# Where three activation tiles start beside their weight tiles, in a two-block float32 kernel

## The chip, the core and the metric

The kernel runs on one core of a Trainium2 chip. The metric is the device time of one launch in microseconds; lower is better. The kernel before took 1932.09 us (median of 3 runs, 1929.77 to 1934.56).

## The reference

Two model blocks run one after the other over 256 tokens of width 1024, in float32. The first has a recurrent layer (a gated linear recurrence beside a state-space part), a gated feed-forward network, an attention layer with three dilated windows, and a second network. The second block has two layers; each multiplies its normed input by a 1024 x 12240 matrix, feeds three branches (latent attention, RWKV, gated linear attention) and merges them. What matters here is that nearly all weight is in plain products. The feed-forward network:

```python
def swiglu_layer(x, norm_g, w_gate_up, w_down):      # 1024 -> 2 x 2816 -> 1024
    h = rmsnorm(x, norm_g)
    g, u = jnp.split(h @ w_gate_up, 2, axis=-1)
    return x + (jax.nn.silu(g) * u) @ w_down
```

and the input of each layer of the second block:

```python
        h = _rms_norm(x, norm_pre[l]) * (1 + scale[:, None, :]) + shift[:, None, :]
        p = h @ w_in[l]
```

## The kernel before

Activations lie features first: a tile of 8 rows of 256 tokens (DK x T, 4 bytes each), so a product is out = weights^T x activations with a 128x128 weight tile held in TensorE (a weight load, PEld) and 256 token columns moving past it (a matmul). Most products are made in three passes of the faster fp32r type: weights and activations are each split into a rounded part ("high") and the rest ("low"), and high x high, high x low and low x high are added in one bank. Each pass loads its weight tile again. In a product "by token" (line 697) the roles are turned: the activations are the held tile and 256 weight columns move.

Weights stream through two layouts. In the layers a weight unit of 8 x 128 columns (UNIT, 4096 bytes a partition) lands in one of five raw buffers, ScalarE or VectorE rounds it into one of three high buffers (lines 722, 717), VectorE writes the low part over the raw one (line 733), and TensorE multiplies (`multiply_unit`, line 708; `first_units_by_pieces`, line 667, for the first two units of a stage). In the two networks (`ffn_pe`) bigger pieces go through two slots of high and low parts in the tile `parts`; the first half of a network (gate and up) multiplies the networks' input rows H_PARTS, the second half (down) the inner rows HIDDEN_PARTS, both by `three_passes` (lines 1486 to 1488) in hardware loops, with the first piece of the first half at line 1501.

Three places are set by constants in words of 4 bytes. X_SHIFT: the layer input HX (high and low) begins that many words after the start of a room behind the high buffers. H_SHIFT: H_PARTS begins that many words behind the weight slots in `parts`. HIDDEN_SHIFT: the same for HIDDEN_PARTS. All rooms, units and slots are multiples of 256 bytes long, so these constants are also the distance, modulo 256 bytes, between any row of the three tiles and any weight tile that it is multiplied with: 64, 64 and 192 bytes.

Used so: HX feeds every three-pass product of the recurrent layer's input and of both layers' inputs in the second block (by token at line 697 for one of them); H_PARTS feeds the networks' first halves and the attention layer's query, key and value products; HIDDEN_PARTS feeds the networks' second halves. By the code's units (24 matmuls to a unit of 8 tiles, 48 to a piece of a network's first half, 132 to a turn of its second half) these are 4968, 2688 and 1056 matmuls, 8712 together, of 10,536 in three passes. The other 1824 (outputs of the branches, expansions of the latent attention) have tiles at other distances, which the change leaves alone: among them the RWKV output (192 bytes), the recurrent layer's second output half (0 and 128) and the last output product of a layer (high part 64, low part 0).

Of the kernel before, what the change touches and what calls it, by code (L numbers as in the profile page):

```python
# [163 lines left out]
def program(nc, A, out, stop=None):  # L164
    with ExitStack() as ctx:
# [16 lines left out]
        KD_ = FFN // P  # L182
        UNIT, RAWS, HIGHS = DK * P, 5, 3
        LINE = 128
        X_SHIFT, H_SHIFT, HIDDEN_SHIFT = (16, 16), (16, 16), (48, 48)
        WHOLE = 2 * KD_ * COLS + 2 * 2 * T + LINE
        SPLIT_AT, SPLIT = COMMON + WHOLE, 2 * 2 * DK * COLS + 2 * DK * T + 2 * KD_ * T + 2 * LINE
        psum = [ctx.enter_context(nc.psum_tensor(f"bank{i}", [P, 512], F32))[:, :] for i in range(8)]
# [3712 lines left out]
```

How the kernel before makes its waits and increments, by code:

```python
        def load_first_up(l):  # L560
            sp.wait_ge(unit_used.sem, last_split[l] + 1)
            for s in range(2):
                for to, frm in ffn_up[l].loads(s, WHOLE_UP[s]):
                    sp.dma_start(to, frm).then_inc(landed[s].sem, 16)
# [1 line left out]
        def load_up(l):  # L567
            job, turns = ffn_up[l], turns_before[l]
            with sp.Fori(1, UPS) as j:
                for s in range(2):
                    sp.wait_ge(lo_ready[s].sem, j + turns)
                    for to, frm in job.loads(j * 2 + s, WHOLE_UP[s]):
                        sp.dma_start(to, frm).then_inc(landed[s].sem, 16)
# [1 line left out]
        def load_down(l):  # L575
            job, turns = ffn_down[l], turns_before[l]
            for q in range(2):
                sp.wait_ge(lo_ready[q].sem, turns + UPS)
                for to, frm in job.loads(q, WHOLE_DOWN[q]):
                    sp.dma_start(to, frm).then_inc(landed[q].sem, 16)
            with sp.Fori(1, DK // 2) as j:
                for q in range(2):
                    sp.wait_ge(lo_ready[1].sem, j * 2 + (turns + UPS + q - 1))
                    for to, frm in job.loads(j * 2 + q, WHOLE_DOWN[q]):
                        sp.dma_start(to, frm).then_inc(landed[q].sem, 16)
# [46 lines left out]
        def load_units(job):  # L632
# [1 line left out]
                u = job.first + i  # L634
                if u >= RAWS:
                    sp.wait_ge(unit_used.sem, u - RAWS + 1)
                for to, frm in job.loads(i, UNIT_RAW[u % RAWS].rearrange("p (k c) -> p k c", k=job.kt)):
```

## Time and profile before

| | |
|---|---|
| median of 3 runs | 1932.09 us |
| profiled execution, its own time | 1930.44 us |
| its span (first to last instruction) | 1927.4 us |
| outside the span | 3.0 us |
| TensorE busy with matmuls | 1849.3 us, 96% |
| VectorE busy | 1339.1 us, 69% |
| ScalarE busy | 814.6 us, 42% |
| mean granted TensorE clock | 0.991 of full |

A matmul's own duration (about 280 ns) is longer than the distance from one to the next (under 120 ns), since they are pipelined. What a product costs is therefore read from how many matmuls start in a stretch: in a window of L microseconds without a stall that is wholly covered, the count holds also those that began up to 0.28 us before it, so the distance is (L + 0.28) / count.

### The profile page before, as it was taken

The numbers are of one execution on the slowest core, as the hardware profiler recorded it, in microseconds if no ns is written. First come the engines' busy times: TensorE is split into PE (matmuls) and PEld (weight loads), VectorE is DVE, ScalarE is ACT, GpSimd is POOL, SyncE is SP. The second block draws the span as 40 slices with busy tenths as digits, with TensorE's granted clock in tenths as the row PEclk, the third lists the DMA queues.
The fourth block names the chain that finished last, engine by engine and source line by source line (L and its number), as shares of the span: only waits on it lengthen the run. The fifth ranks groups of instructions, "written<-read, shape, count | busy, mean of one in ns | idle before, by whom it ended". The sixth has DMA issues, their size and how long they took to land.

```text
span 1927.4 us, 42678 instructions
## 1 busy us (share of the span) xinstructions
PE 1849.3 (96%) x18447; PEld 1728.3 (90%) x18447; DVE 1339.1 (69%) x1723; ACT 814.6 (42%) x1219; POOL 88.3 (5%) x131
## 2 busy tenths in 40 slices
PE   8999999999899999999998999998999999999999
PEld 7987999998689999998987799897998997889988
DVE  8897688757748876764786469666774696459755
ACT  5573534435634342223755234254213664235154
POOL 2000000000400000002000000000002000000000
PEclk9999999999999999999999999999999999999999
DMA  8555477974337795663550145554563651135644
GB/s 224 144 144 152 129 264 257 271 201 137 105 99 250 264 267 136 164 174 94 163 153 15 47 119 165 145 146 128 145 185 88 163 154 47 28 105 160 172 118 134
DMA packets 473228, 291.94 MB, mean 151 GB/s; under 512 B 26775, under 2 KB 467580, under 8 KB 472872
## 3 DMA queue, kind: packets, MB, share of 16 engines
q1 hardware_dynamic: 466720, 262.13, 48.5%
q0 software_dynamic: 5312, 25.32, 3.5%
q10 hardware_dynamic: 1032, 2.11, 0.5%
q8 instruction: 126, 2.06, 0.5%
q14 instruction: 38, 0.31, 0.1%
HBM read 287.95 MB, written 1.05 MB: 150 GB/s over the span
## 4 chain that ended last, share of the span: by engine, by line
PE 79%; DVE 14%; ACT 4%; issue 2%; DMA 1%; ACTq 0%; POOL 0%; DVEq 0%
PE bank L708 37%; PE bank L1486 6%; PE bank L1488 6%; PE bank L1487 6%; DVE rounded L733 4%; PE bank L667 3%; PE bank L949 3%; PE bank L697 2%; ACT rounded L722 1%; PE bank L1692 1%; PE bank L1679 1%; PE bank L1116 1%; DVE rounded L717 1%; PE bank L790 1%; PE bank L941 1%
## 5 line engine op out<-in xcount | busy, mean ns | idle before, releaser
L708 PE MATMUL bank<-rounded 128*128 128x256 f32 x5928 | 719.1, 281 | 10.2 <-DVE rounded L733 7.9
L708 PEld LDWEIGHTS bank<-rounded 128*128 128x128 f32 x5928 | 700.8, 187 | 25.2 <-DVE rounded L733 12.3
L733 DVE TENSOR_TENSOR rounded<-arena,rounded 128x1024 fp32r<-128x1024 f32 (+1 forms) x307 | 370.6, 1215 | 102.5 <-ACT rounded L722 94.6
L1486 PE MATMUL bank<-parts 128*128 128x256 f32 x1024 | 287.2, 280 | 1.0 <-DVE parts L2323 0.9
L1488 PE MATMUL bank<-parts 128*128 128x256 f32 x1024 | 285.9, 279 | 0.0
L1487 PE MATMUL bank<-parts 128*128 128x256 f32 x1024 | 285.6, 279 | 0.0
L722 ACT ACTIVATE rounded<-arena 128x1024 fp32r<-128x1024 f32 x192 | 201.5, 1057 | 170.2 <-PE bank L708 103.5
L1486 PEld LDWEIGHTS bank<-parts 128*128 128x128 f32 x1024 | 192.8, 188 | 2.2 <-issue 1.2
L1488 PEld LDWEIGHTS bank<-parts 128*128 128x128 f32 x1024 | 192.3, 188 | 0.0
L1487 PEld LDWEIGHTS bank<-parts 128*128 128x128 f32 x1024 | 192.1, 188 | 0.1
L773 ACT ACTIVATE arena<-bank 128x512 f32<-128x512 f32 x90 | 53.2, 596 | 241.6 <-PE bank L708 227.7
L2395 ACT ACTIVATE parts<-whole 128x2048 fp32r<-128x2048 f32 x44 | 84.3, 1918 | 126.9 <-PE bank L1488 109.4
L717 DVE CAST rounded<-arena 128x1024 fp32r<-128x1024 f32 (+1 forms) x115 | 78.2, 680 | 69.2 <-PE bank L708 43.0
L2315 DVE TENSOR_TENSOR parts<-whole,parts 128x2048 fp32r<-128x2048 f32 x44 | 100.7, 2292 | 16.8 <-ACT parts L2395 16.1
L708 PE MATMUL bank<-arena 128*128 128x256 f32 x416 | 91.1, 379 | 0.0
L949 PE MATMUL bank<-common,arena 128*128 128x128 f32 x519 | 78.1, 285 | 13.3 <-DMA common<-in_const 7.1
L708 PEld LDWEIGHTS bank<-arena 128*128 128x128 f32 x416 | 78.9, 190 | 11.5 <-issue 1.0
L708 PE MATMUL bank<-common,arena 128*128 128x256 f32 x384 | 87.8, 383 | 0.0
L708 PEld LDWEIGHTS bank<-common,arena 128*128 128x128 f32 x384 | 71.2, 189 | 10.9 <-issue 0.3
L949 PEld LDWEIGHTS bank<-common,arena 128*128 128x128 f32 x519 | 58.6, 145 | 23.0 <-DMA common<-in_const 7.1
L2323 DVE TENSOR_TENSOR parts<-whole,parts 128x1408 fp32r<-128x1408 f32 x32 | 52.0, 1625 | 38.9 <-ACT parts L2427 38.8
L2427 ACT ACTIVATE parts<-whole 128x1408 fp32r<-128x1408 f32 x32 | 44.1, 1380 | 65.9 <-PE bank L1488 54.5
(407 smaller groups left out, 2405.8 us busy)
## 6 DMA issues: line engine op xcount, KB each, us to landing
arena<-in_w_in SPq DMA_DIRECT2D x190, 512.0 KB, 3.8
whole<-in_ffn_w_gate_up SPq DMA_DIRECT2D x44, 1024.0 KB, 5.2
arena<-in_ada_w POOLq DMA_DIRECT2D x32, 768.0 KB, 6.4
whole<-in_ffn_w_down SPq DMA_DIRECT2D x16, 1408.0 KB, 7.2
arena<-in_rec_w_in SPq DMA_DIRECT2D x36, 512.0 KB, 3.8
arena<-in_att_w_qkv SPq DMA_DIRECT2D x24, 512.0 KB, 3.8
arena<-in_rec_w_out SPq DMA_DIRECT2D x16, 512.0 KB, 3.7
arena<-in_mla_w_o SPq DMA_DIRECT2D x16, 512.0 KB, 3.7
```

The source lines that it names most:

```text
L667: last = pe.matmul(psum[s][:, i * T:i * T + T], w[a][:, kk, :], job.rhs[b][:, kk, :], start=(i, kk, a, b) == (0, 0, 0, 0), stop=kk == job. ...
L708: last = pe.matmul(psum[s][0:c, m % 2 * T:m % 2 * T + T], w[a][:, k, cols], x[b][:, k, :], start=(k, a, b) == (0, 0, 0), stop=k == job.kt ...
L717: write(high_view(job_of[u], u), raw_view(job_of[u], u, UNIT_RAW)).then_inc(done.sem, 1)
L722: high_parts(act, lambda to, frm: act.activation(to, frm, ACT.Copy), high_by_act[0].pop(0), unit_high_s)
L733: dve.tensor_tensor(raw_view(job_of[u], u, UNIT_LOW), raw, high_view(job_of[u], u).bitcast(F32), ALU.subtract)\
L773: return lambda i, bank, done, rounds: act.activation(two(dst, i, lo), bank, func).then_inc(done, 1)
L949: last = pe.transpose(bank[:, n * P:n * P + P], x, ident)
L1486: pe.matmul(bank, w_hi, x_hi, start=start and k == 0, stop=False)
L1487: pe.matmul(bank, w_hi, x_lo, start=False, stop=False)
L1488: last = pe.matmul(bank, w_lo, x_hi, start=False, stop=stop and k == n - 1)
L2315: dve.tensor_tensor(UP_W[s][1], WHOLE_UP[s], UP_W[s][0].bitcast(F32), ALU.subtract)\
L2395: act.activation(UP_W[s][0], WHOLE_UP[s], ACT.Copy)\
```

## The change

Three constants change. X_SHIFT goes from 16 to 12 words (64 to 48 bytes), H_SHIFT from 16 to 4 (64 to 16 bytes), HIDDEN_SHIFT from 48 to 52 (192 to 208 bytes), each for the high and the low part alike. Every instruction, its size and its place in each engine's order stay; only the start addresses of HX, H_PARTS and HIDDEN_PARTS change, for those who write them (ScalarE and VectorE) and for TensorE, which reads them. All starts stay multiples of 16 bytes; they are no longer multiples of 64.

```diff
--- before.py
+++ after.py
@@ -182,7 +182,7 @@
         KD_ = FFN // P
         UNIT, RAWS, HIGHS = DK * P, 5, 3
         LINE = 128
-        X_SHIFT, H_SHIFT, HIDDEN_SHIFT = (16, 16), (16, 16), (48, 48)
+        X_SHIFT, H_SHIFT, HIDDEN_SHIFT = (12, 12), (4, 4), (52, 52)
         WHOLE = 2 * KD_ * COLS + 2 * 2 * T + LINE
         SPLIT_AT, SPLIT = COMMON + WHOLE, 2 * 2 * DK * COLS + 2 * DK * T + 2 * KD_ * T + 2 * LINE
         psum = [ctx.enter_context(nc.psum_tensor(f"bank{i}", [P, 512], F32))[:, :] for i in range(8)]
```

## Rows read from the trace of the kernel before

**Rows 1.** The page: span, engines, TensorE's granted clock by slice.

```profile
span 1927.4 us, 42678 instructions
...
PE 1849.3 (96%) x18447; PEld 1728.3 (90%) x18447; DVE 1339.1 (69%) x1723; ACT 814.6 (42%) x1219; POOL 88.3 (5%) x131
...
PEclk9999999999999999999999999999999999999999
```

**Rows 2.** The page's chain that ended last: shares by line.

```profile
PE bank L708 37%; PE bank L1486 6%; PE bank L1488 6%; PE bank L1487 6%; DVE rounded L733 4%; PE bank L667 3%; PE bank L949 3%; PE bank L697 2%; ACT rounded L722 1%; PE bank L1692 1%; PE bank L1679 1%; PE bank L1116 1%; DVE rounded L717 1%; PE bank L790 1%; PE bank L941 1%
```

**Rows 3.** Groups by line and shape, TensorE (count; busy, mean ns; idle before).

```profile
L708 PE MATMUL bank<-rounded 128*128 128x256 f32 x5856 | 710.8, 281 | 10.2 <-DVE rounded L733 7.9 <-ACT arena L773 1.6 <-ACT common L3280 0.6
L1486 PE MATMUL bank<-parts 128*128 128x256 f32 x1024 | 287.2, 280 | 1.0 <-DVE parts L2323 0.9
L708 PE MATMUL bank<-arena 128*128 128x256 f32 x416 | 91.1, 379 | 0.0
```

**Rows 4.** Windows without a stall, TensorE: stretch, length, busy (count), clock, DMA.

```profile
core 0: us, PE busy (x), PEclk, DMA share, GB/s
233.00:333.00 100.00, 100.00 (x852) 1.00 0.74 252
353.00:368.00 15.00, 15.00 (x134) 1.00 1.05 312
675.50:684.50 9.00, 9.00 (x82) 1.00 1.01 270
693.00:743.00 50.00, 50.00 (x427) 1.00 0.98 277
789.50:801.00 11.50, 11.50 (x104) 1.00 0.51 141
1381.00:1398.00 17.00, 17.00 (x147) 1.00 0.64 168
1173.00:1181.00 8.00, 8.00 (x73) 1.00 0.66 193
195.50:206.00 10.50, 10.50 (x91) 1.00 0.66 189
1315.00:1328.00 13.00, 13.00 (x111) 1.00 0.79 220
```

**Rows 5.** Timeline, one network's first half, then second half, TensorE.

```profile
239.84 0.28 PE L1488 MATMUL bank<-parts 128*128 128x256 f32 x1
239.95 0.28 PE L1486 MATMUL bank<-parts 128*128 128x256 f32 x1
...
359.96 0.28 PE L1487 MATMUL bank<-parts 128*128 128x256 f32 x1
360.07 0.28 PE L1488 MATMUL bank<-parts 128*128 128x256 f32 x1
```

**Rows 6.** Windows over three of eight quick stretches of moved products, TensorE.

```profile
137.40:142.60 5.20, 5.20 (x49) 1.00 0.53 158
352.40:399.60 47.20, 47.20 (x413) 1.00 1.03 302
...
1795.40:1817.00 21.60, 21.60 (x193) 1.00 0.70 187
```

**Rows 7.** Windows over three networks' halves: length, then PE PEld DVE ACT POOL, clock, DMA.

```profile
220.50:346.20 125.70, 125.61 (x1062) 125.27 (x1060) 96.00 (x86) 49.23 (x39) 5.28 (x10) 1.00 0.70 235
346.20:407.80 61.60, 61.24 (x528) 60.68 (x529) 43.91 (x40) 28.36 (x28) 7.02 (x8) 1.00 0.93 271
...
685.80:748.80 63.00, 62.44 (x530) 62.27 (x530) 43.15 (x36) 23.56 (x19) 2.11 (x4) 1.00 0.86 243
```

**Rows 8.** Waits of TensorE: total us, times, longest.

```profile
PE bank L708 <- DVE rounded L733: 9.0, 13, 1.4
```

**Rows 9.** Timeline, two full-precision stages with other row positions, TensorE.

```profile
151.78 1.46 PE L708 MATMUL bank<-arena 128*128 128x256 f32 x6
...
997.76 2.11 PE L708 MATMUL bank<-common,arena 128*128 128x256 f32 x9
```

## Prediction

> **What bounds the kernel now.** I read the page first. TensorE is busy for 96% of the 1927.4 us span, and its granted clock is the full level, 2.4 GHz, in all 40 slices [rows 1]. In the chain that ended last, line 708 holds 37% of the span and the three passes of the networks 6% each [rows 2]. So the end is set by how fast one three-pass matmul follows the other, and by little else: the largest wait of TensorE behind the product stream, that for VectorE's low parts, is 9.0 us in 13 waits [rows 8]. Two of the groups show the size of the stream: 5856 matmuls at line 708 take 710.8 us, 121.4 ns each with all their small stops, and each of the three passes of the networks has 1024 [rows 3].
>
> The change moves no instruction. It can act only through the distance between matmuls, so the reader has to look at that distance by stage. From the windows (length plus 0.28 us, over the count) it comes out in two levels [rows 4]:
>
> - first network's first half (64 bytes): 100.28 / 852 = 117.7 ns
> - the same network's second half (192 bytes): 15.28 / 134 = 114.0
> - end of the second network's first half (64): 9.28 / 82 = 113.2
> - second network's second half (192): 50.28 / 427 = 117.8
> - two stages on HX (64): 11.78 / 104 = 113.3 and 17.28 / 147 = 117.6
> - RWKV output, not moved (192): 8.28 / 73 = 113.4
> - recurrent output (128 and 0): 10.78 / 91 = 118.5
> - a layer's last product (high 64, low 0): 13.28 / 111 = 119.6
>
> The timeline shows the same at single matmuls: starts at 239.84 and 239.95 in the one, and at 359.96 and 360.07 in the other, where over a longer run the first goes at about 118 and the second at about 113 [rows 5].
>
> Two things follow. One distance knows two steady levels, 113.3 (quick) and 117.8 (slow): the same code at the same addresses ran its second half quick in the first network and slow in the second. So something other than the address picks the level, and it holds until the stream is interrupted. But the address has a part in it. Where 0 or 128 is mixed in, I find neither level but 118.5 and 119.6, and by length the quick level is far more common at 192 than at 64. Eight quick stretches of the moved products hold 1,271 matmuls, from the one at 137.4 to the one at 1795.4; the longest, 413 matmuls in 47.2 us with its small stops, is a second half at 192 [rows 6].
>
> **The change part by part.** Removed and added instructions: none. Written tiles: ScalarE and VectorE write HX, H_PARTS and HIDDEN_PARTS as often and as long as before; I cost their new starts at nothing, since VectorE is busy for only 96.0 of the 125.7 us of a network's first half [rows 7], and if it did get slower there it has 30 us of room. Moved reads: 4968 matmuls on HX, 2688 on H_PARTS, 1056 on HIDDEN_PARTS, 8712 in all. About 1,271 of them are quick and 7,441 slow.
>
> *Does a start off a multiple of 64 bytes cost by itself?* The full-precision stages answer for starts inside the granule. At 152 us the tokens' rows start at 48 past a multiple of 64 (by the layout), and six records take 1.46 us; the last has its own 379 ns at the end [rows 3], so (1.46 - 0.38) / 5 = 216 ns. At 998 us the rows start 12 past one, and nine take 2.11 us: (2.11 - 0.38) / 8 = 216 ns [rows 9]. That stream needs its rows at half the rate, so it bounds the cost only for a slow reader: from below 0, from above unknown. I take 0 and keep in the range one quarter of the step between the levels, 1.1 ns x 8712 = 10 us.
>
> *Which level do the moved streams take?* No row shows 48, 16 or 208. The nearest rows are 64, 192 and 0. They bound one matmul from both sides. Below: the quick level everywhere, 7,441 x (117.8 - 113.3 = 4.5 ns) = 33 us gained. Above: the price of 0. In the last product one matmul in three has 0, so it costs (119.6 - 117.7) x 3 = 5.7 ns. Weighed by nearness to 0, that is 1.4 ns for HX (48 lies three quarters of the way to 64), 4.3 for H_PARTS (16), 1.4 for HIDDEN_PARTS (208): 4968 x 1.4 + 2688 x 4.3 + 1056 x 1.4 = 7.0 + 11.6 + 1.5 = 20 us, and the quick matmuls of today would be lost too, 1,271 x 4.5 = 5.7 us: 26 us lost.
>
> Between these ends I choose the side of the quick level. All distances met so far are multiples of 64 bytes, and at those the stream sits on the edge between two levels: the same addresses give both. Which of two steady patterns comes out is then a matter of how the weight reads and the token reads fall between each other in time; a distance inside the granule shifts one against the other by a part of a step, and a tie that the grid of 64 leaves open need not be open there. I take two thirds of the moved matmuls as quick: 5,808 - 1,271 = 4,537 more, x 4.5 = 20 us. This is a choice, not a reading.
>
> *What is given back.* A quicker TensorE meets its suppliers earlier. The two second halves price it: the one that was mostly quick (413 x 4.5 = 1.9 us to gain) took 61.6 us, the slow one 63.0 [rows 7], so 1.4 of 1.9 us was kept, three quarters. The rest is late weights: DMA was busy 0.93 of that window. Of 20 us I keep 15. From the profiled execution's own 1930.4 us (1.7 below the median) that gives 1915 us.
>
> The page "SBUF — State Buffer" of the Trainium skill says in "Who interferes with whom" that TensorE has two independent read ports, one for the moving operand and one for the weight load, and waits on nobody. By it the distance could not matter and the sum would be 0. The rows at mixed 0 and 128 stand against it, the two levels at one address stand beside it unexplained.
>
> **The rivals.** *Nothing happens* (1931): the level is picked by the moment of the last interruption alone, and the address is only along for the ride. For it: quick and slow at the same 64 and at the same 192. Against it: the second halves and the branch outputs at 192 are quick so much more often. Each interruption draws anew, so the sum would wander by a few us: 1925 to 1937. It is also what the page's rule would give.
>
> *The tiles come too close to their weights* (slower, 1946). One mechanism: the nearer to a distance of 0, the more often the token read meets the weight read in the same place, as in the last product. It bites at H_PARTS first, at 16 bytes, which is all of the networks' first halves. Its full price is the 26 us above; since the recurrent output, with 0 in a third of its matmuls too, shows 118.5 and not 119.6 (0.8 x 3 = 2.4 ns in place of 5.7, under half), I take three fifths, 16 us. It decides from the point where a matmul at 16 bytes costs over 1 ns. For it: both stages with 0 are above both levels. Against it: only about a third of the sum is from distances that were seen, and 48 and 208 are still nearer to the old places.
>
> *Everything gets quick* (1905): 33 us, three quarters kept, 25 us. I count it to my forecast's case, at its edge.
>
> *A third level below 113.3* (about 1865): 256 columns at 2.4 GHz are 106.7 ns, so up to 7,441 x 11 + 1,271 x 6.6 = 90 us, three quarters kept. For it only that 113.3 is itself not the floor; no row of this type shows less.
>
> **How the numbers follow.** Quick for a good part of the moved matmuls: 0.44 (1905 to 1924). A third level: 0.05. Nothing: 0.23. Too close: 0.28. What a measurement of this kernel can tell from no change is about 0.3%, 6 us. Faster: 0.42 of the first case, 0.05, and 0.03 of wandering, 0.50; same: 0.02 + 0.18 + 0.02 = 0.22; slower: 0.02 + 0.26 = 0.28. The range leaves out the third level, the upper end of the full price at 0, and takes in the rest: 1897 to 1948. The likeliest case's own range is 1905 to 1924.
>
> **What would show it.** Right: windows in the networks' first halves (both slow now for nearly their whole 125 us) with counts near 883 in 100 us in place of 852, their length near 121 us, and HX stages at 113.3; waits for VectorE's low parts a little above 9 us. Wrong in the choice: counts of 852 again, or new distances of 118.5 and more, most of all in the first halves at 16 bytes. Wrong in the give-back: quick windows everywhere, but the halves no shorter. If HX, H_PARTS and HIDDEN_PARTS answer differently, the three distances have to be told apart, and my one share for all of them was wrong. VectorE's and ScalarE's mean durations should not move at all.

## The result, and the profile after

The changed kernel is slower: 1936.57 us (median of 11 runs, 1932.37 to 1941.55) against 1929.89 for the kernel before in its 11 runs; ratio 1.0031, 95% interval 1.0021 to 1.0042. The forecast was 1915, in a range of 1897 to 1948. Four executions in the groups below, two of them of the kernel before, took 2650 to 6351 us and are left out of every ratio.

Page of the changed kernel: span, busy times of the engines, chain that ended last by line.

```profile
span 1934.8 us, 42678 instructions
...
PE 1858.8 (96%) x18447; PEld 1739.4 (90%) x18447; DVE 1339.2 (69%) x1723; ACT 815.1 (42%) x1219; POOL 88.3 (5%) x131
...
PE bank L708 39%; PE bank L1486 6%; PE bank L1488 6%; PE bank L1487 6%; DVE rounded L733 3%; PE bank L949 3%; PE bank L667 3%; PE bank L697 2%; PE bank L1692 1%; PE bank L1679 1%; PE bank L1116 1%; ACT rounded L722 1%; DVE rounded L717 1%; PE bank L1660 1%; PE bank L941 1%
```

Against [rows 1] TensorE is busy for 9.5 us more and idle for 76.0 us in place of 78.1; 9.5 - 2.1 = 7.4 us, which is the whole growth of the span. VectorE, ScalarE and GpSimd are busy as before to within 0.5 us. In the chain line 708 grows from 37% to 39% [rows 2].

Groups by line and shape, and the wait that [rows 8] shows, after:

```profile
L708 PE MATMUL bank<-rounded 128*128 128x256 f32 x5856 | 716.3, 283 | 9.3 <-DVE rounded L733 7.2 <-ACT arena L773 1.6 <-ACT common L3280 0.6
L1486 PE MATMUL bank<-parts 128*128 128x256 f32 x1024 | 288.4, 282 | 1.1 <-DVE parts L2323 1.1
L708 PE MATMUL bank<-arena 128*128 128x256 f32 x416 | 91.1, 379 | 0.0
```

```profile
PE bank L708 <- DVE rounded L733: 7.9, 11, 1.4
```

The same 5856 matmuls take 5.5 us more than in [rows 3], the full-precision ones exactly as long as before, and the wait for VectorE's low parts is shorter, 7.9 us in place of 9.0, as it would be if TensorE comes later and finds its suppliers in time more often.

Windows without a stall after, TensorE: stretch, length, busy (count), clock, DMA share, GB/s.

```profile
229.00:265.00 36.00, 36.00 (x311) 1.00 0.65 216
270.00:330.00 60.00, 60.00 (x508) 1.00 0.73 250
356.00:378.00 22.00, 22.00 (x187) 1.00 0.96 287
423.00:435.00 12.00, 12.00 (x108) 1.00 0.62 182
570.00:670.00 100.00, 100.00 (x845) 1.00 0.70 241
693.00:749.00 56.00, 56.00 (x472) 1.00 0.91 257
793.00:811.00 18.00, 18.00 (x154) 1.00 0.57 157
```

With the formula of [rows 4] the first network's first half (H_PARTS at 16 bytes) runs at 116.7 ns, then at 118.7; the second network's at 118.7 (845 matmuls in 100 us, where the kernel before had 852 and the forecast wanted 883); the second halves (208 bytes) at 119.1 and 119.2; attention's first product on H_PARTS (16) at 113.7; a stage on HX (48) at 118.7, which is 118.35 by its starts. The granted clock is 1.00 in all of them, 2.4 GHz. So these are new levels, not a new mix of the two old ones.

**The granted clock.** It is not at the full level throughout. The page's digits hide it, but the trace of the kernel before has six short stretches, 34 us together, at 0.50 (1.2 GHz), in which three-pass matmuls start 213 ns apart. One of them begins at 756.5 us, after TensorE had run 48 matmuls of one column each (line 1551, from 752.3 us on), and covers a layer's first products; below it an equal length at 1.00:

```profile
756.60:763.30 6.70, 6.70 (x32) 0.50 0.06 20
1380.00:1386.70 6.70, 6.70 (x60) 1.00 0.44 108
```

The profiled execution of the changed kernel has 34 us of this too, so the busy times above compare fairly. Over all executions the mean clock is 0.9903 for the changed kernel and 0.9917 for the 29 of the kernel before that ran beside the first experiments. Within the groups an execution with 0.001 less of clock takes about 0.9 us more, so some 1 us of the 7 may be the clock's; this is an estimate from these numbers. Why the clock fell a little more often is not shown.

The networks' halves after: length, then PE PEld DVE ACT POOL, clock, DMA.

```profile
220.90:346.90 126.00, 126.00 (x1062) 125.65 (x1061) 96.08 (x85) 49.19 (x38) 5.28 (x10) 1.00 0.71 235
346.90:411.10 64.20, 63.67 (x533) 63.29 (x532) 44.05 (x40) 28.45 (x28) 7.01 (x8) 1.00 0.89 259
687.40:751.30 63.90, 63.37 (x532) 63.20 (x531) 43.15 (x36) 23.60 (x19) 2.11 (x4) 1.00 0.84 238
```

By the first and last start the two second halves take 63.8 and 63.6 us; before, 61.5 and 62.9 [rows 7]. The new distance explains it: 528 x 119.17 ns = 62.9 us, and the rest is small stops.

**Where the time went, by tile.** One matmul more or less in a window of 18 us is 0.8 ns, which is too coarse. For the tables I took from the trace's records every three-pass matmul whose next three follow without a pause, and averaged the distance of their starts; the stretches at 1.2 GHz are left out. "Quick" is the share within 1.7 ns of 113.3.

| stream | matmuls | before: distance, ns, quick | after | sum |
|---|---|---|---|---|
| HX | 4584 | 64: 117.28, .11 | 48: 118.26, .01 | +4.5 us |
| HX by token (roles turned) | 384 | 192: 115.08, .61 | 208: 118.05, 0 | +1.1 |
| H_PARTS, networks | 2112 | 64: 117.58, .04 | 16: 118.33, 0 | +1.6 |
| H_PARTS, attention | 384 | 64: 117.78, 0 | 16: 115.86, .46 | -0.7 |
| H_PARTS, attention by token | 192 | 192: 114.75, .68 | 240: 118.34, 0 | +0.7 |
| HIDDEN_PARTS | 1056 | 192: 115.92, .42 | 208: 119.15, 0 | +3.4 |

Together +10.6 us of stream, of which the span shows 7.4. The streams that were not moved agree: 117.56 and 117.78 at 64, 116.01 and 116.16 at 192. A single short stream wanders more, though: the RWKV output, at 192 in every kernel that leaves the weight units in place, has quick shares from .18 to .98 (before .49, after .35). In the product by token the weight columns move and the activations are held, so the distance has the other sign; the prediction counted these 576 matmuls with the rest and did not say so. The 4584 on HX also hold 72 with weight tiles of only 16 columns, whose distances run through the multiples of 64.

### The profile page after: what moved, and what is told of

It is laid out like the page before. It is cut to its first block, busy times and chain, and to the rows that moved or that the text cites. A ratio compares the mean times of both kernels' runs of the same rounds, so it can differ in the third digit from the quotient of the medians.

```text
span 1934.8 us, 42678 instructions
## 1 busy us (share of the span) xinstructions
PE 1858.8 (96%) x18447; PEld 1739.4 (90%) x18447; DVE 1339.2 (69%) x1723; ACT 815.1 (42%) x1219; POOL 88.3 (5%) x131
## 4 chain that ended last, share of the span: by engine, by line
PE 80%; DVE 12%; ACT 3%; issue 2%; DMA 1%; ACTq 0%; POOL 0%; DVEq 0%
PE bank L708 39%; PE bank L1486 6%; PE bank L1488 6%; PE bank L1487 6%; DVE rounded L733 3%; PE bank L949 3%; PE bank L667 3%; PE bank L697 2%; PE bank L1692 1%; PE bank L1679 1%; PE bank L1116 1%; ACT rounded L722 1%; DVE rounded L717 1%; PE bank L1660 1%; PE bank L941 1%
## 5 line engine op out<-in xcount | busy, mean ns | idle before, releaser
L717 DVE CAST rounded<-arena 128x1024 fp32r<-128x1024 f32 (+1 forms) x115 | 78.1, 679 | 73.1 <-PE bank L708 43.6
```

The costliest lines, as they stand in the source:

```text
L717: write(high_view(job_of[u], u), raw_view(job_of[u], u, UNIT_RAW)).then_inc(done.sem, 1)
```

## The experiments

All of them move tiles and no instruction. Where there is an interval, the kernel before ran beside it in the same rounds.

### One tile at a time

```diff
-        X_SHIFT, H_SHIFT, HIDDEN_SHIFT = (16, 16), (16, 16), (48, 48)
+        X_SHIFT, H_SHIFT, HIDDEN_SHIFT = (12, 12), (16, 16), (48, 48)   # only HX, 48 bytes
+        X_SHIFT, H_SHIFT, HIDDEN_SHIFT = (16, 16), (4, 4), (48, 48)     # only H_PARTS, 16
+        X_SHIFT, H_SHIFT, HIDDEN_SHIFT = (16, 16), (16, 16), (52, 52)   # only HIDDEN_PARTS, 208
```

> Only the layer input HX moves (64 to 48 bytes); H_PARTS stays at 64, HIDDEN_PARTS at 192. Theory A (each stream's level is set by its own distance): every stall-free window on HX shows 118.3 ns between matmuls in place of 117.8 or 113.3, all else as before; 4968 x 0.55 ns = 2.7 us, and about 700 quick matmuls lost x 5 ns = 3 us: 5 to 6 us slower, ratio about 1.003, nearly all of the change. Rival (the levels are redrawn by chance at each stall, the distance only rides along): HX windows show 113.3 or 117.8 again in other places, and the ratio lies within 1.001 of 1.

> Only the networks' input H_PARTS moves (64 to 16 bytes). Theory A: in the networks' first halves neither 117.8 nor 113.3 shows, but the new levels of 16 bytes, 116.7 and 118.7; per network half (1056 matmuls) between -1.2 and +0.9 us. Since 118.7 holds for longer, in all -1 to +2 us, ratio 1.000 to 1.001. It is also the part whose runs spread most (116.7 against 118.7 over 2016 matmuls is 4 us). Rival (chance alone): 117.8 as before over nearly all of both first halves, ratio 1.000.

> Only the inner rows HIDDEN_PARTS move (192 to 208 bytes). Theory A: both second halves run at about 119 ns and never at 113.3; against before 1056 x 1.3 ns = 1.4 us and 413 quick matmuls more x 4.4 ns, three quarters of it kept: together 2 to 3 us slower, ratio 1.0013. Rival (chance alone): one second half or both show 113.3 stretches again, ratio within 1.001 of 1.

| moved alone | median, us | before, us | ratio, 95% interval |
|---|---|---|---|
| HX to 48 | 1934.42 | 1929.29 | 1.0025 [1.0016, 1.0034] |
| H_PARTS to 16 | 1929.58 | 1929.29 | 0.9999 [0.9988, 1.0010] |
| HIDDEN_PARTS to 208 | 1932.18 | 1929.29 | 1.0018 [1.0008, 1.0028] |

The parts' sum is 1.0042, the whole 1.0031, within each other's intervals. HX has 118.26 ns again, with no quick stretch, as theory A has it. H_PARTS, the tile nearest to its weights, costs nothing here. Its windows say why; networks with H_PARTS alone at 16:

```profile
229.00:265.00 36.00, 36.00 (x311) 1.00 0.67 222
268.00:323.00 55.00, 55.00 (x460) 1.00 0.74 250
326.00:345.00 19.00, 19.00 (x170) 1.00 0.88 271
568.00:604.00 36.00, 36.00 (x311) 1.00 0.65 219
630.00:672.00 42.00, 42.00 (x362) 1.00 0.75 255
```

116.7, 120.2, 113.4, 116.7 and 116.8 ns: at 16 bytes the same loop knows four levels (118.7 is the fourth, after), changes between them where the stream is interrupted, and here they average 117.45, about as 64 bytes did (117.58). The expectation had left out 113.3 and 120.0, and in the trace of the change, where 118.7 held for longer, the same distance had 118.33. With HIDDEN_PARTS alone at 208, the second halves:

```profile
356.00:371.00 15.00, 15.00 (x128) 1.00 1.02 302
695.00:749.00 54.00, 54.00 (x465) 1.00 0.93 261
```

119.4 and 116.7 ns: two levels again, neither of them 113.3; the expectation had about 119 for both.

### All three at 192

```diff
+        X_SHIFT, H_SHIFT, HIDDEN_SHIFT = (48, 48), (48, 48), (48, 48)
```

> HX, H_PARTS and HIDDEN_PARTS all stand at 192 bytes, a multiple of 64 (so HX and H_PARTS move from 64). Theory A (distance 192 reaches the quick level more readily than 64): more than half of the moved matmuls at 113.3, that is some 3500 more x 4.4 ns, three quarters kept: 10 to 13 us faster, ratio 0.994. Rival (level redrawn by chance at stalls, the same for 64 and 192): about one in seven quick as before, ratio within 1.001 of 1.

1921.98 us, ratio 0.9959 [0.9943, 0.9976]: faster than both kernels, though by 7 us and not by the 10 to 13 expected. Its page and four windows (first network's first half, second network's, its second half, a stage on HX):

```profile
span 1918.9 us, 42678 instructions
...
PE 1835.6 (96%) x18447; PEld 1714.3 (89%) x18447; DVE 1338.1 (70%) x1723; ACT 815.0 (42%) x1219; POOL 88.3 (5%) x131
```

```profile
229.00:345.00 116.00, 116.00 (x987) 1.00 0.73 244
632.00:682.00 50.00, 50.00 (x444) 1.00 0.81 267
690.00:745.00 55.00, 55.00 (x469) 1.00 0.92 258
765.00:783.00 18.00, 18.00 (x161) 1.00 0.77 181
```

117.8, 113.2, 117.9 and 113.5 ns: only the two old levels, but mixed otherwise. HX has 114.84 ns with .66 quick (64 gave .11), the networks' first halves 116.68 with .25. TensorE's busy time falls by 13.7 us and the span by 8.5, 62%; some 1.5 us of either is the clock, which is at 1.2 GHz for 31 us here and for 34 before (an estimate from the two distances, 213 and 118 ns). Its wait for the low parts is longer:

```profile
PE bank L708 <- DVE rounded L733: 11.2, 19, 1.5
```

### Distance or start?

The change moves two things at once: the distance and the place of the rows in the granule of 64 bytes. Two kernels keep one of them. All unit buffers of the layers start 48 bytes past a multiple of 64 and HX 64 bytes behind them (first), or the unit buffers start at 16 and HX at 48 bytes behind, so that its rows are on a multiple of 64 (second).

```diff
+        OFF = [0]
...
-            place[0] += (COMMON - place[0]) % 16
+            place[0] += (COMMON + OFF[0] - place[0]) % 16
...
+        OFF[0] = 12        # second: 4, and X_SHIFT = (12, 12)
```

> The weight units of the layers start 48 bytes past a multiple of 64, and HX with them (112 bytes past), so their distance stays 64 as before while the rows of HX start off a multiple of 64, as after the change. H_PARTS in its own products with `parts` and HIDDEN_PARTS are untouched. Theory A (the distance between row and weight tile decides): windows on HX show 117.8 or 113.3 ns as before. Rival (a row that starts off a multiple of 64 bytes is read more slowly): 118.3 ns in every window on HX, and no 113.3.

> The counterpart: the weight units start 16 bytes past a multiple of 64 and HX at a multiple of 64, which makes the distance 48 while the rows are aligned. Theory A: 118.3 ns in every stall-free window on HX and no 113.3. Rival (row start decides): 117.8 or 113.3. A third outcome, the weight tile's own start deciding, would show the same in both of these kernels, unlike before.

One execution each, 1928.33 and 1930.49 us, beside 1927.92 for the kernel before. The first stage on HX has 432 matmuls that the timeline merges into one row (start, length; less 0.28 us, over 431, it is the distance). In turn: before, the change, HX alone at 192, distance 64 off the granule, distance 48 on it, and 0 (below).

```profile
27.53 51.05 PE L708 MATMUL bank<-rounded 128*128 128x256 f32 x432 [0.63 <-DVE rounded L733]
```
```profile
27.68 51.27 PE L708 MATMUL bank<-rounded 128*128 128x256 f32 x432 [0.59 <-DVE rounded L733]
```
```profile
27.57 49.25 PE L708 MATMUL bank<-rounded 128*128 128x256 f32 x432 [0.94 <-DVE rounded L733]
```
```profile
27.42 49.23 PE L712 MATMUL bank<-rounded 128*128 128x256 f32 x432 [0.94 <-DVE rounded L737]
```
```profile
27.58 50.59 PE L712 MATMUL bank<-rounded 128*128 128x256 f32 x432 [0.81 <-DVE rounded L737]
```
```profile
27.52 51.94 PE L708 MATMUL bank<-rounded 128*128 128x256 f32 x432 [0.49 <-DVE rounded L733]
```

117.8, 118.3, 113.6, 113.6, 116.7 and 119.9 ns, short stops included. The last 24 of the 432 are matmuls with 16-column tiles, which keep 113.3 to 113.7 ns in all six kernels; without them the slow ones are 0.2 to 0.4 ns higher. Neither kernel does what either of its expectations said. Distance 64 has its quick level off the granule too, at 113.6; but its slow level is then 118.3 and not 117.8 (HX over all stages: .24 quick, mean 117.15). Distance 48 with rows on the granule has no quick level, but 116.7 in place of 118.3 (once 120.0, for 119 matmuls). Attention's products with H_PARTS, which are at the same distance 48 with rows on the granule in this kernel, have 116.69 too. So at these two distances the quick level goes with the distance, and the height of the others with distance and start together. Whether the rows' start or the weights' start does it is not separated: both kernels move the weights' start too.

### More distances

```diff
+        X_SHIFT, H_SHIFT, HIDDEN_SHIFT = (0, 0), (0, 0), (64, 64)      # 0, 0, 0 bytes
+        X_SHIFT, H_SHIFT, HIDDEN_SHIFT = (32, 32), (32, 32), (16, 16)  # 128, 128, 64
+        X_SHIFT, H_SHIFT, HIDDEN_SHIFT = (8, 8), (40, 40), (56, 56)    # 32, 160, 224
+        X_SHIFT, H_SHIFT, HIDDEN_SHIFT = (56, 56), (8, 8), (40, 40)    # 224, 32, 160
```

> All three at a distance of 0 modulo 256 bytes (HIDDEN_PARTS at 256). My prediction priced 0 at 5.7 ns over the slow level from a stage with 0 in one matmul of three; if that holds, all three show 121 to 124 ns and the whole is 30 to 50 us slower, and the level rises steadily from 64 over 48 and 16 to 0. Rival (theory B: each distance has levels of its own that do not lie on a slope, as 16 bytes with 116.7, 118.7 and 120.0 already suggests): a level at 0 that is not above 120, under 20 us slower.

> HX and H_PARTS at 128 bytes, HIDDEN_PARTS at 64. Theory A: HX and H_PARTS take a level of their own, slower than at 64 or 192 (the recurrent output, with 128 in two matmuls of three, has 118.8): 118 to 121 ns, 5 to 20 us in all; HIDDEN_PARTS at 64 shows 117.8 or 113.3. Rival (chance at stalls): the two old levels in their old shares.

> HX at 32 bytes, H_PARTS at 160, HIDDEN_PARTS at 224: three distances that no run has shown, all with row starts off a multiple of 64. If a quick level (113.3) needs a distance of 64 or 192 exactly, as before, after and the runs so far suggest, none of the three shows a steady 113.3 and each stream's mean lies between 116.5 and 120, about 118.5; the whole about 8 us slower. Rival (a smooth slope from 0 and 128, the slowest, to 64 and 192, the quickest): 32 between 118 and 119.5, 160 and 224 near 117 with a share of quick matmuls, the whole within 3 us of before.

> The same three distances on the other tiles: HX at 224, H_PARTS at 32, HIDDEN_PARTS at 160. If the level belongs to the distance and not to the stage, each shows about the mean that it shows in the kernel beside this one, within 0.7 ns; if stage and distance act together (the weights of a network's first half lie in steps of 1024 bytes, the units' in steps of 512), the means differ by more. The whole 5 to 12 us slower than before; a smooth slope would make it 0 to 4 us.

One execution each: 1947.99 and 1940.81 us beside 1927.92; 1930.39 and 1937.04 beside 1929.79. These times carry the clock as well, 0.989, 0.990, 0.993 and 0.988 beside 0.992 and 0.990: by the 0.9 us for 0.001 above, 3 of the 20 us at 0, and some 4 of the 7 us between the last two. What follows rests on the distances, not on the times. Windows in the networks, first halves and then second, with all at 0:

```profile
230.00:348.00 118.00, 118.00 (x986) 1.00 0.73 242
700.00:755.00 55.00, 55.00 (x461) 1.00 0.92 256
```

with 128 and 64:

```profile
232.00:348.00 116.00, 116.00 (x980) 1.00 0.74 245
696.00:751.00 55.00, 55.00 (x469) 1.00 0.93 262
```

with 160 (both first halves) and 224:

```profile
228.00:347.00 119.00, 119.00 (x994) 1.00 0.73 242
570.00:687.00 117.00, 117.00 (x988) 1.00 0.74 243
696.00:750.00 54.00, 54.00 (x459) 1.00 0.93 260
```

with 32 (both first halves):

```profile
232.00:324.00 92.00, 92.00 (x791) 1.00 0.72 242
570.00:629.00 59.00, 59.00 (x504) 1.00 0.69 233
```

120.0 and 119.9; 118.7 and 117.9; 120.0, 118.7 and 118.3; 116.7 and 117.6 ns. The levels of all runs, from stretches of over 80 matmuls, weights on the granule, and the mean distance of whole tiles, one number for each trace and tile:

| distance, bytes | levels seen, ns | means of HX and the networks' tiles, ns |
|---|---|---|
| 0 | 120.0 | 119.8, 120.0, 120.0 |
| 16 | 113.3, 116.7, 118.7, 120.0 | 118.33, 117.45 |
| 32 | 116.7, 117.8 | 116.93, 117.20 |
| 48 | 118.3 | 118.26, 118.26 |
| 64 | 113.3, 117.8 | 117.18 to 117.79 |
| 128 | 118.7, 120.0 | 119.04, 118.67 |
| 160 | 117.3, 118.7, 120.0 | 119.30, 118.97 |
| 192 | 113.3, 117.8 | 114.2 to 117.7 |
| 208 | 116.7, 119.2 | 119.15, 117.92 |
| 224 | 118.3 | 118.32, 118.26 |

Each of 32, 160 and 224 was measured on two tiles, in code of different form, and the two agree within 0.4 ns. At all three the rows start 32 bytes past a multiple of 64, so their start alone does not set the mean either (117, 119 and 118.3). One tile at one distance can differ as much from trace to trace (1.2 ns at 208, 0.9 at 16), so that the set of levels goes with the distance and not with the stage is likely, but rests on few traces. A slope towards 0 there is not: 32 is among the best, 160 is above 128, and 0 is 2.2 ns above 117.8. The expectation of 121 to 124 ns and 30 to 50 us at 0 was too high, and so was that of 8 us for 32, 160 and 224, which cost 0.6 in its one execution.

### How much is the draw?

The quick share at an unchanged distance wanders from kernel to kernel, so a difference of 0.3% could be luck. The control moves everything behind the common block by 64 bytes, and with it rows and weights alike. One stream is an exception: in the recurrent layer's second output half the high weights are placed from the arena's end and stay, and its 118.84 ns become 117.78. Another kernel moves HX alone to 192.

```diff
-        COMMON = CONST.shape[1] + PACKS * P + 2 * DK * T + 6 * T + 4 + 56
+        COMMON = CONST.shape[1] + PACKS * P + 2 * DK * T + 6 * T + 4 + 72
...
-        assert base == COMMON
+        base = place[0] = COMMON
```

```diff
+        X_SHIFT, H_SHIFT, HIDDEN_SHIFT = (48, 48), (16, 16), (48, 48)
```

> Every tile behind the common block stands 64 bytes further on, rows and weights alike, so all distances, and all starts modulo 64, are those of the kernel before; only the absolute places differ. This is a control on how far the time wanders when the stages draw their levels anew. Theory A (the distance sets which levels are open to a stage, the last interruption picks one of them): the same levels 113.3 and 117.8 on HX, H_PARTS and HIDDEN_PARTS, none of 118.3 or 119, with the quick share of single stages shuffled; time 1925 to 1934 against 1929.9, mean distance of the stream within 0.3 ns of 117.15. Rival B (the absolute place matters, so the 0.3% of the change could be any move's): new levels in these stages, a mean distance above 117.6 or below 116.7 and a time outside of 1925 to 1934.

> HX alone at 192 bytes from its weights, H_PARTS at 64 and HIDDEN_PARTS at 192 as in the kernel before. Theory A (192 opens the quick level more often than 64 does, matmul by matmul; HX went from 117.28 to 114.84 ns with all three at 192): HX near 114.8 again, 4968 x 2.4 ns = 12 us of stream, two thirds of it kept, so about 1922, equal to all three at 192. Rival B (the quick share in that run was a lucky draw): HX's mean distance 116 or more with a quick share under 0.4, time 1926 or more.

Control: 1931.25 us against 1928.56, ratio 1.0014 [1.0001, 1.0026]. Its first network's first half and second network's second half:

```profile
260.00:345.00 85.00, 85.00 (x724) 1.00 0.77 257
695.00:750.00 55.00, 55.00 (x469) 1.00 0.94 259
```

117.8 and 117.9 ns, and no level of 118.3 or more in any stretch; what changed is the quick share (HX .05, HIDDEN_PARTS .02 where it was .42), and the mean of the moved tiles is 117.49 in place of 117.06, a little more than the 0.3 ns I had allowed. The draw alone is thus worth up to some 3 us, 1 of which goes with a lower clock (0.9906 against 0.9917); the interval excludes 1, although no distance of the moved tiles changed. The change has 118.28, so of its 1.22 ns some 0.8 are new levels, and 0.4 could be had from an unlucky draw at the old ones.

HX alone at 192: 1923.49 us, ratio 0.9971 [0.9961, 0.9981]; HX 114.51 ns, .73 quick. Three groups of executions that differ in nothing but HX's distance: 48 is 1.0025, 64 is 1, 192 is 0.9971. That most of the gain at 192 repeats, with a high quick share in both profiles (.66 and .73) where 64 had .05 to .13 in four traces and, off the granule, .24, speaks against a lucky draw. Over HX and the networks' tiles, 64 has 0 to .13 in ten cases, and 192 has .02 to .81 in nine, seven of them over .2. A single tile can still be lucky: HIDDEN_PARTS, at 192 and not moved, has .81 in the kernel that moves only HX and .02 in the control. Whether the other two tiles add anything at 192 (0.9959 against 0.9971) the intervals do not settle.

## Why the prediction was wrong

- *What bounds the kernel*: right in the main. TensorE's granted clock was read as full throughout, and is 1.2 GHz for 34 us; in the profiled pair this does not differ. The span follows TensorE's busy time: -13.7 us gave -8.5 (all at 192), +9.5 gave +7.4 (the change), +21.4 gave +18.8 (all at 0, busy 1870.7 and span 1946.2; some 3 us of both is the clock, 41 us at 1.2 GHz).
- *"One distance knows two steady levels, 113.3 (quick) and 117.8 (slow)"*: true of 64 and 192 and of no other distance measured. The prediction read two distances, both a multiple of 64 but not of 128, and took their pair of levels for the stream's own. The rows that were neither (118.5 and 119.6, with 0 and 128 mixed in [rows 4]) were the sign that other distances have levels of their own; 0 and 128 show 120.0 and 118.7.
- *The step that failed: the choice of "the side of the quick level" for 48, 16 and 208 bytes, "two thirds of the moved matmuls as quick", 4,537 x 4.5 = 20 us gained.* Measured: +10.6 us of stream. At 48 and 208 there is no quick stretch of over 80 matmuls, at 16 there are short ones (95 matmuls after, 170 in a window with H_PARTS alone); most of the stream took levels of 118.3, 118.7 and 119.2, which the prediction did not have. The 1,271 quick matmuls were not joined by 4,537; all but some 180 of attention's were lost. The step had no row beside it and said so; the argument for it (an open tie is decided by an offset) held neither in sign nor in kind. Part of the loss is luck: the control lost 0.43 of the 1.22 ns by the draw alone.
- *A start off a multiple of 64 taken at 0*: wrong by half a nanosecond. At the same distance of 64, the slow level off the granule is 118.3 in place of 117.8; and at distance 48, rows on it and weights off it, 116.7. The full-precision stages, which need their rows at half the rate, could not show it. The 1.1 ns kept in the range covers the first and not the second, 1.6 ns.
- *Give-back, three quarters kept*: near enough where the stream got slower (7.4 of 9.5, 78%), too much where it got quicker: 8.5 of 13.7 (62%), and 4.3 of 10.0 with HX alone at 192 (span 1923.1, busy 1839.3). These are pairs of single executions, and a kernel's executions scatter by several us, so the shares are rough. One network's half did not give the price in the layers, where TensorE meets VectorE's low parts: its wait for them was 11.2 us with all at 192, against 9.0, which is 2.2 of the 5.2 us not kept.
- *The rival "too close to the weights", 1946*: the right sign, the wrong mechanism. It was to bite first at 16 bytes, which alone costs nothing (0.9999); the loss lies at 48 (1.0025) and 208 (1.0018). Its full price, 5.7 ns at 0, is 2.2 ns by the run with all at 0. It was worked out of the last product's 119.6, a count of 111, where one matmul more or less is 1.1 ns. By the starts of the same matmuls the distance is 118.9, which would have given 3.3 ns.
- *"Nothing happens", 1925 to 1937*: its wandering is real, some 3 us, and the time fell within it by its edge; but new levels in the windows exclude it as the cause.
- The Trainium skill's page "SBUF — State Buffer", in "Who interferes with whom", has TensorE's two read ports independent and TensorE waiting on nobody. The 20 us between all at 0 and the kernel before (17 without the clock's share) say that the place of moving rows against held weights matters here, by whatever way; by that rule all of these kernels would have had one time.

## What to carry to other kernels

When one engine's stream is the bound, the steady distance between two of its instructions is the quantity to read, to a tenth of a nanosecond, and by stage; a mean duration hides it. Where a mean holds several levels, find out which settings open which levels before forecasting a mix, and price an unseen setting from both sides rather than by the mechanism one would like. Here, rows and weight tiles 192 bytes apart modulo 256 were best, 0 was worst and 128, 160 and 208 were next, and a control that moves everything by the same amount showed how much of a small difference is luck. The granted clock has to be compared too, execution by execution.

## What the runs showed of the hardware

- A stream of fp32r matmuls of 128x128 by 256 columns, each with its own weight load, at a granted clock of 1.00 (2.4 GHz), has steady distances of 113.33, 116.67, 117.78, 118.33, 118.67 and 120.00 ns: 272, 280, 282.7, 284, 284.8 and 288 cycles. Beside them, stretches of over 80 matmuls had 119.15 (208 bytes), once 117.3 (160) and once 123.2 (a product by token at 208, at 116 to 117 and 130 ns in turn); none is below 113.3, 16 cycles above the 256 columns.
- A level is the mean of a pattern that repeats. In the records, which have whole nanoseconds, the distances come back within 1 ns after 3 matmuls at 113.33 (340 ns for the three), after 9 at 117.78 (1060 ns), 12 at 118.33 (48 bytes, 1420 ns), 15 at 118.67 (16 bytes, 1780 ns) and 24 at 119.17 (208 bytes, 2860 ns); at 120.00 each is 120. One mean can come from two patterns: 116.67 is 119 to 120 and 114 in turn at 16 bytes, and 117, 116, 117 at 32.
- A level holds for hundreds of matmuls (1004 at 118.67 in one network's half at 128 bytes) and changes at an interruption. Which one is drawn is not fixed by the distance: 16 bytes gave 116.7, 120.0 and 113.3 in a row in one loop.
- The draw depends on the distance: over the profiles with HX at 192 the quick share is .66 and .73, at 64 it is .05 to .13.
- At a granted clock of 0.50 (1.2 GHz) the same matmuls start 213 ns apart; the traces have 27 to 48 us of it.

What makes the patterns and their levels, banks of the buffer, the order in which row and weight reads take turns, or something else, is open: no run here separates these. A layer's last product, with one matmul in three at 0 and the others at 64, has a pattern of its own, 118.9 ns in the window of [rows 4]: five distances of 116 to 119 ns and one of 126 to 128.
